# Down projections of three feed-forward groups as seven half-size products in place of eight, on one Trainium2 core

## What is computed

```python
h = rms_norm(x, g_mlp[layer])
x = x + jnp.square(jax.nn.relu(h @ w_up[layer])) @ w_down[layer]
```

## Time and profile before

| | |
|---|---|
| median of 3 runs (lowest to highest) | 1565.25 us (1564.1 to 1566.73) |
| the profiled execution's own time | 1565.43 us |
| its span, first to last instruction | 1563.8 us |
| mean granted TensorE clock | 0.992 of full speed |
| PE, PEld, DVE, ACT, POOL busy | 1515.2, 1422.2, 726.7, 492.3, 117.9 us |
| feed-forward part, in the order of MLP_ORDER | 382 to 789 us (layer 0), 1138 to 1549 us (layer 1) |

### The profile page before, as it was taken

How to read it: one execution, slowest core, us unless ns; L and a number is a source line. 1 busy time by engine, 2 the same in 40 slices (tenths; PEclk the granted TensorE clock), 3 DMA queues, 4 the chain that set the end, 5 groups by cost and what they waited for, 6 DMA issues and landing times.

```text
span 1563.8 us, 33452 instructions
## 1 busy us (share of the span) xinstructions
PE 1515.2 (97%) x13119; PEld 1422.2 (91%) x13119; DVE 726.7 (46%) x1273; ACT 492.3 (31%) x787; POOL 117.9 (8%) x238
## 2 busy tenths in 40 slices
PE   6999999989999999999999999998999999999996
PEld 5999866779999999999999997667999999999996
DVE  4355475635444343343543476774544434334333
ACT  5111154423432132231321115552333313213133
POOL 5310112210000000000010000222000000000000
PEclk9999999999999999999999999999999999999998
DMA  4323477833222223222242227775222222322222
GB/s 132 99 77 83 132 255 246 262 105 90 82 80 86 76 84 91 80 81 83 78 146 84 81 73 248 241 264 156 81 81 82 81 84 77 94 79 83 81 81 75
DMA packets 230949, 178.84 MB, mean 114 GB/s; under 512 B 9320, under 2 KB 202924, under 8 KB 230850
## 3 DMA queue, kind: packets, MB, share of 16 engines
q1 hardware_dynamic: 217154, 137.50, 30.0%
q0 software_dynamic: 13696, 40.00, 8.0%
HBM read 170.20 MB, written 7.26 MB: 113 GB/s over the span
## 4 chain that ended last, share of the span: by engine, by line
PE 90%; DVE 3%; ACT 2%; SPq 2%; issue 2%; DMA 1%; POOLq 0%; POOL 0%; ACTq 0%; DVEq 0%
PE B L1316 71%; PE B L1533 3%; PE B L1342 2%; PE B L1545 2%; PE B L1333 1%; PE B L1627 1%; PE B L1565 1%; PE B L1589 1%; PE B L1576 1%; SPq L382 1%; DMA WR<-in_w_in_even_dram 1%; PE B L1543 1%; PE B L1415 1%; PE B L1486 1%; DVE KP L1162 1%
## 5 line engine op out<-in xcount | busy, mean ns | idle before, releaser
L554 ACT ACTIVATE WH<-WR 128x1024 fp32r<-128x1024 f32 x175 | 184.5, 1054 | 436.6 <-PE B L1316 423.9
L822 DVE TENSOR_TENSOR WL<-WR,WH 128x1024 fp32r<-128x1024 f32 x188 | 230.2, 1224 | 57.6 <-ACT WH L544 28.9
L1316 PE MATMUL B<-ffH,WH 128*128 128x288 f32 x1024 | 218.9, 294 | 0.0
L1316 PE MATMUL B<-ffL,WH 128*128 128x288 f32 x1024 | 218.6, 294 | 0.0
L1316 PE MATMUL B<-ffH,WL 128*128 128x288 f32 x1024 | 217.7, 294 | 0.0
L1316 PE MATMUL B<-H2L,WH 128*128 128x288 f32 x960 | 205.0, 294 | 0.0
L1316 PE MATMUL B<-H2H,WH 128*128 128x288 f32 x960 | 204.7, 294 | 0.0
L1316 PE MATMUL B<-H2H,WL 128*128 128x288 f32 x960 | 204.1, 294 | 0.0
L1316 PE MATMUL B<-HH,WH 128*128 128x288 f32 x832 | 179.9, 298 | 4.2 <-DVE WL L822 2.6
L856 DVE TENSOR_TENSOR X<-B,X 128x288 f32 (+1 forms) x160 | 66.0, 453 | 242.4 <-PE B L1316 242.0
L1316 PE MATMUL B<-HL,WH 128*128 128x288 f32 x832 | 178.6, 296 | 0.0
(11 more groups left out here) (299 smaller groups left out, 1689.3 us busy)
## 6 DMA issues: line engine op xcount, KB each, us to landing
WR<-in_w_up_dram SPq DMA_DIRECT2D x64, 512.0 KB, 4.1
WR<-in_w_down_dram SPq DMA_DIRECT2D x64, 512.0 KB, 3.8
KRX<-in_cache_fox_k_dram SPq DMA_DIRECT2D x48, 256.0 KB, 4.2
WR<-in_w_in_odd_dram SPq DMA_DIRECT2D x24, 512.0 KB, 3.7
KRX<-in_cache_sb_k_dram SPq DMA_DIRECT2D x48, 256.0 KB, 3.8
VR<-in_cache_fox_v_dram POOLq DMA_DIRECT2D x44, 256.0 KB, 4.1
VR<-in_cache_sb_v_dram POOLq DMA_DIRECT2D x44, 256.0 KB, 4.7
WR<-in_w_in_even_dram SPq DMA_DIRECT2D x20, 512.0 KB, 3.9
```

Source lines behind the costliest of these rows:

```text
L554: A(WH[1 - u][:], WR[1 - u][:], ACT.Copy).then_inc(S["w_high"], 1)
L822: V.tensor_tensor(WL[u][:], WR[u][:], WH[u][:].bitcast(F32), ALU.subtract).then_inc(S["w_low"], 1)
L1316: last = M(B[2 * u + h][:, 0:TH], w[u][:, k, :], x[:, k, h * TH:(h + 1) * TH], start=(k == 0 and n == 0), stop=(k == KT - 1 and n == 2))
```

## The change

MLP_ORDER becomes up 0, seven 0, up 1, seven 1, up 2, seven 2, up 3, down 3. A "seven" is a down group done as 2 x 2 block products: two output blocks (m) against the even and odd blocks of the contraction (e) against the two row halves. The eight block products are replaced by seven of sums of blocks (Winograd's form of Strassen's scheme). A seven has NQ = 4 pairs q, each with its own 1 MB of weights; every product is 4 blocks k x 3 partial products = 12 matmuls 128x128 on 128x288 into one bank. Group 3 stays as it was, directly behind its up group.

- Weights of a pair: SP loads them (`load_pair`) into ZR or, for odd q, into both WR buffers (WRP has their address). GpSimd makes four sums of 128x512 per pair (S1 to S4). ScalarE makes the high part (`block_high`, 128x512, seven per pair) and VectorE the low part (`block_low`). The first pair's sums wait until unit 4 of the up group is done.
- Operands: after an up unit VectorE and ScalarE make the blocks and their sums T1 to T4 (`evac_ops`). Even units (u = 0) have T1 to make, odd ones T2, T3 and T4. Both unit-weight cuts of a turn of the loop are in the odd unit's body.
- Results: VectorE adds each product to 1 to 4 blocks of X (`add_product`: 1152, 576, 288, 864, 288, 576 and 288 elements).
- Buffers OPH, OPL and FR lie where ffH and ffL were, ZH, ZL and ZR where HH and HL were. Some semaphores are merged; G_MLP counts (FG + 1) * KT units per layer in place of 2 * FG * KT.

```diff
+        PRODUCTS = [("11", OP_11), ("S1", OP_T1), ("12", OP_21), ("S2", OP_T2), ("S4", OP_22), ("S3", OP_T3), ("22", OP_T4)]
+        def product_bank(q, i):
+            return B[(4 + 7 * q + i) % 8]
...
+                def load_pair(L, grp, q):
+                    Q = pair_no(L, grp, q)
+                    if Q >= 2:
+                        sp.wait_ge(S["block_low"], 7 * (Q - 1))
+                    sp.dma_start((ZR if q % 2 == 0 else WRP)[:, :, :], dn_v[L][grp][:, :, 2 * P * q:2 * P * (q + 1)]
+                                 ).then_inc(S[f"pair_in{q % 2}"], 16)
...
+                    if kind == "seven":
+                        for q in range(1, NQ):
+                            if q == 1:
+                                sp.wait_ge(S["w_low"], g + 2)
+                            load_pair(L, grp, q)
+                        sp.wait_ge(S["block_low"], 7 * (pair_no(L, grp, NQ - 1) + 1))
+                        continue
...
+                        unit_loop(sp, load, g, 4)
...
+                        load_pair(L, grp, 0)
+                        unit_loop(sp, load, g + 4, KT - 4, i0=4)
...
+                        pool.wait_ge(S[f"pair_in{q % 2}"], 16 * (Q // 2 + 1))
+                        if q == 0:
+                            pool.wait_ge(S["unit_done"], G_MLP[L] + grp * KT + 6)
+                        if Q >= 1:
+                            pool.wait_ge(S["block_low"], 7 * (Q - 1) + 2)
+                        g.tensor_tensor(s1, a21, a22, ALU.add).then_inc(S["w_sum"], 1)
+                        if Q >= 1:
+                            pool.wait_ge(S["block_low"], 7 * (Q - 1) + 4)
+                        pool.wait_ge(S["w_sum"], 4 * Q + 1)
+                        g.tensor_tensor(s2, s1, a11, ALU.subtract).then_inc(S["w_sum"], 1)
+                        if Q >= 1:
+                            pool.wait_ge(S["product"], 7 * (Q - 1) + 5)
+                        pool.wait_ge(S["w_sum"], 4 * Q + 2)
+                        g.tensor_tensor(s4, a12, s2, ALU.subtract).then_inc(S["w_sum"], 1)
+                        if Q >= 1:
+                            pool.wait_ge(S["product"], 7 * (Q - 1) + 6)
+                        g.tensor_tensor(s3, a11, a21, ALU.subtract).then_inc(S["w_sum"], 1)
...
+            def block_high(Q, i):
...
+                if Q >= 1:
+                    act.wait_ge(S["product"], 7 * (Q - 1) + i + 1)
+                A(ZH[:, i], block_src(Q, i), ACT.Copy).then_inc(S["block_high"], 1)
...
+                        up_loop(act, body, g + first, first, (KT - 2 - first) // 2)
+                        body(g + KT - 2, KT - 2, NQ - 1, 0, None)
+                        for i in range(5):
+                            block_high(Q, i)
+                        body(g + KT - 1, KT - 1, NQ - 1, 1, None)
+                        block_high(Q, 5)
+                        block_high(Q, 6)
...
+            def evac_ops(L, grp, b0=0, z=None):
...
+                    dve.wait_ge(S["unit_done"], g + 2)
+                    f0 = FR_11 if u == 0 else FR_21
+                    for h in range(2):
+                        done = V.scalar_tensor_tensor(FR[:, f0 + h], B[b0 + 2 * u + h][:, 0:TH], 0.0, R[:, h * TH:(h + 1) * TH], ALU.max, ALU.mult)
+                    done.then_inc(S["relu_scaled"], 1)
+                    dve.wait_ge(S["relu_squared"], i + (m0 + 1))
+                    if u == 0:
+                        V.tensor_tensor(FR[:, FR_T1], FR[:, FR_12], FR[:, FR_11], ALU.subtract).then_inc(S["op_sums"], 1)
+                    else:
+                        V.tensor_tensor(FR[:, FR_T2], FR[:, FR_22], FR[:, FR_T1], ALU.subtract).then_inc(S["op_sums"], 1)
+                        V.tensor_tensor(FR[:, FR_T3], FR[:, FR_22], FR[:, FR_12], ALU.subtract)
+                        dve.wait_ge(S["op_sums"], j * 3 + (3 * j0 + 2))
+                        V.tensor_tensor(FR[:, FR_T4], FR[:, FR_21], FR[:, FR_T2], ALU.subtract).then_inc(S["op_sums"], 1)
+                        low_ops(OP_21, OP_22, FR_21, j, j * 3 + (3 * j0 + 2)).then_inc(S["op_half"], 1)
+                        if more in ("behind", "both"):
+                            cut_low(g + 2, 1)
+                    lo, hi, f = (OP_T1, OP_11, FR_T1) if u == 0 else (OP_T2, OP_T4, FR_T2)
+                    low_ops(lo, hi, f, j, j * 3 + (3 * j0 + (1 if u == 0 else 3))).then_inc(S["evac_dve"], 1)
...
+                        for q in range(NQ):
+                            Q = pair_no(L, grp, q)
+                            for i in range(7):
+                                add_product(Q, q, i)
+                                if q < NQ - 1:
+                                    block_low(Q + 1, i)
+                                elif i == 5:
+                                    cut_low(g, 0)
+                                elif i == 6 and grp + 1 < FG - 1:
+                                    cut_low(g + 1, 1)
...
+                        body(g + KT - 2, KT - 2, NQ - 1, 0, None)
+                        for i in range(5):
+                            block_low(Q, i)
+                        body(g + KT - 1, KT - 1, NQ - 1, 1, None)
+                        block_low(Q, 5)
+                        block_low(Q, 6)
...
+            def seven(L, grp, q, g):
+
+                Q = pair_no(L, grp, q)
+                J = pair_no(L, grp, NQ)
+                for i, (name, op) in enumerate(PRODUCTS):
+                    pe.wait_ge(S["block_low"], 7 * Q + i + 1)
+                    if i == 0 and q == 0:
+                        pe.wait_ge(S["evac_dve"], g + 1)
+                        if Q > 0:
+                            pe.wait_ge(S["product_read"], 7 * Q)
+                    if 7 * q + i >= 8:
+                        pe.wait_ge(S["product_read"], 7 * Q + i - 7)
+                    if q == 0 and name == "12":
+                        pe.wait_ge(S["op_half"], J)
+                    if q == 0 and name == "S2":
+                        pe.wait_ge(S["evac_dve"], g + 2)
+                    for k in range(NQ):
+                        for n, (w, x) in enumerate(((ZH, OPH), (ZH, OPL), (ZL, OPH))):
+                            done = M(product_bank(q, i)[:, 0:TH], w[:, i, k, :], x[:, op, k, :], start=(k == 0 and n == 0), stop=(k == NQ - 1 and n == 2))
+                    done.then_inc(S["product"], 1)
```

More of the change, by code:

```diff
@@ L785, in _ @@
                     last = L == 1 and n == len(MLP_ORDER) - 1
-                    if kind == "down" and grp == FG - 1:
+                    if kind == "seven":
+                        for q in range(1, NQ):
+                            for i in range(7):
+                                block_high(pair_no(L, grp, q), i)
+                        cut_high(g)
+                        if grp + 1 < FG - 1:
+                            cut_high(g + 1)
+                        continue
+                    if kind == "down":
                         for i in range(KT):
                             evac_sq(2 + 2 * L)(g + i, i, i % 2, None if last and i == KT - 1 else "next")
+                    elif grp == FG - 1:
+                        unit_loop(act, evac_up(L, grp), g, KT)
                     else:
-                        body = evac_up(L, grp) if kind == "up" else evac_none
+                        body, Q = evac_ops(L, grp), pair_no(L, grp, 0)
                         if n == 0:
@@ L1319, in unit, with late_chunk_unit @@
                 return body
+            def seven(L, grp, q, g):
+                Q = pair_no(L, grp, q)
+                J = pair_no(L, grp, NQ)
[15 more added lines that the diff above has]
+                    done.then_inc(S["product"], 1)
+            def late_chunk_unit(hi, lo, g):
+                pe.wait_ge(S["w_low"], g + 3)
+                pe.wait_ge(S["evac_dve"], g + 1)
+                for k in range(KT):
+                    if k == KT - 1:
+                        pe.wait_ge(S["evac_dve"], g + 2)
+                    for n, (w, x) in enumerate(((WH, hi), (WH, lo), (WL, hi))):
+                        for h in range(2):
+                            last = M(B[h][:, 0:TH], w[0][:, k, :], x[:, k, h * TH:(h + 1) * TH],
+                                     start=(k == 0 and n == 0), stop=(k == KT - 1 and n == 2))
+                last.then_inc(S["unit_done"], 1)
             def turn_y(k):
@@ L1699, in _ @@
                 g = G_MLP[L]
-                up_end = {}
                 for n, (kind, grp) in enumerate(MLP_ORDER):
+                    if kind == "seven":
+                        for q in range(NQ):
+                            seven(L, grp, q, g)
+                        pe.wait_ge(S["product_read"], 7 * pair_no(L, grp, NQ - 1) + 3)
+                        continue
                     if kind == "up":
```

185 lines of the change are left out of this document (147 added, 38 removed).

## The result

The changed kernel takes 1550.72 us (median of 5 runs, 1548.81 to 1552.88) beside 1565.56 us of the kernel before (5 runs, 1564.1 to 1566.73): a ratio of 0.9903, 95% interval 0.9893 to 0.9914. Forecast were 1545 us and a range of 1532 to 1561. The profiled execution took 1550.72 us, its span is 1549.1 us.

What follows compares the result with a forecast made beforehand. TensorE was taken to set the time. Of 38.1 us saved by fewer matmuls, waits of 0.6, 1.9 and 0.5 us in six groups give back 18, a gain of 20.1: 1545 us, range 1532 to 1561.

Steps and rivals of the forecast that it cites:

- The saving: Six sevens issue 288 fewer matmuls at an unchanged 132.2 ns each: 38.1 us less.
- (b): Start of the seven: TensorE waits 1.3 us for operands plus 0.6 for pair 1's sums colliding with VectorE, 1.9 us per group.
- (a): Unit 6 of the up group: GpSimd's first-pair sums collide with VectorE; wait between 0 and 1.2 us, 0.6 taken.
- (c): End of the seven: the next up unit's weight cut stands behind the sixth product's add; TensorE waits 0.5 us per group.
- Inside a seven: no gap: Per pair of 11.1 us, VectorE needs 9.0 us, ScalarE 4.4 and GpSimd 5.1, so TensorE never waits mid-seven.
- slack of "about 5 us": Inside a seven, VectorE may lag about 5 us, from when low parts are due and banks are reused.
- The path behind it: Seven's end: next up group's loads wait until pair 3 is cut, about 11 us before the end, and need 4.1 us.
- Nothing holds VectorE: Rival: sums never delay VectorE, unit 6 waits 0 and the seven's start 1.3 us; 1538 us, chance 0.27.
- Held whole at the ends: Rival: each sum holds VectorE whole; waits 1.2 at unit 6, 3.7 and 0.5 at seven's ends; 1559.5 us, chance 0.17.
- the 1.3 given as a sign of being right: Sign for the forecast: GpSimd's 96 sums would take near 1.3 us each.
- the 1.8 given as a sign of being wrong: Sign against the forecast: GpSimd sums above 1.8 us.
- the 1.84 at which the gain would have been used up: Slow-sums rival, chance 0.12: from 1.84 us per GpSimd sum the kernel gains nothing; at 2.2 us, 1578 us.

Runs made afterwards that it cites:

- run 1: Changed kernel with GpSimd's four sums left out, their blocks cut from raw block 11 by ScalarE and VectorE instead: 1537.59 us.
- Run 6: Changed kernel with VectorE cutting the next up group's first weights after the fifth add of the last pair, not the sixth: 1547.66 us.
- run 5: Changed kernel with pair 1's sums held until VectorE ends the up group's evacuation, and four weight blocks instead of five before unit 7's evacuation: 1557.78 us.
- run 7: Changed kernel with the edits of run 4, run 5 and Run 6 together: 1554.39 us.
- run 2: Changed kernel with GpSimd's sums replaced by fills of a spare buffer, 1.06 us each, which write and read nothing: 1536.94 us.
- run 4: Changed kernel with the first pair's sums split over two gates, two behind unit 2 and two behind unit 4: 1545.15 us.
- run 9: Changed kernel with the edits of run 4 and Run 6 together, pair 1's sums and blocks unchanged: 1542.38 us.
- run 10: Kernel of run 7 with the last pair's weight blocks made ahead of the later adds in each seven's third pair: 1552.3 us.
- run 11: Kernel of run 9 with four blocks between units 6 and 7 and the last pair's blocks ahead of the adds: 1550.48 us.
- run 3: Changed kernel with every GpSimd sum done twice, one after the other: 1624.27 us.

## Why the prediction was right, point by point

**The saving** of 288 matmuls at 132.2 ns, 38.1 us, stands: neither the waits before each product nor twelve matmuls in one bank slowed them. **(b), the third product**, was put at 1.9 us and is 1.83, but that is luck: its two parts are mis-sized against each other. Without the sums it is 0.73 (run 1), not 1.3; there VectorE ends the evacuation of unit 6 at 432.52, 3.5 us after that unit and not 4.0, and is hardly late to unit 7. And the one block of the five that a sum holds (1.79 us, 0.69 free) adds 1.10, not 0.6.

**(a), unit 6**, was mis-sized: 0.6 taken, the middle of 0 to 1.2; measured 1.13 at five groups. Step by step the working holds: VectorE is held for 1.55 - 0.46 and 2.21 - 1.23, together 2.07 us, and had 0.95 us to spare, which leaves 1.12. What failed is the choice of the middle: at five groups T1 and the cut both came behind a sum that had begun, by 0.05 us in T1's case; at the sixth T1 came first, and the wait is nothing. Each tie goes one way or the other, and no place shows the middle.

**(c), behind the seven**, was 0.5 and is 0.64 to 0.79; it is the same without sums, so it is the add and the cut in line, as put, with a handover more. Run 6 removes it at five of six places.

With the measured waits the sum gives 1565.4 - 38.1 + 20.6 = 1547.9 us; 1.85 of what is left came ahead of the feed-forward part, and the last 1 us is about what steps a little longer than the pace add up to (3.0 us in the feed-forward parts, 1.3 before).

**Inside a seven: no gap** is right in its outcome and wrong in its reason. The 9.0 us of VectorE's work are right (9.15 without sums), but the holds fill the pair to 11.10 of 11.10. The slack of "about 5 us" is thus no reserve: it can be spent once, and runs 5 and 7 spent it. The path behind it was too short as well: pair 3 was to be cut 11 us before the seven ends, and in the trace its last block ends at 475.77, some 7 us before.

**The rivals.** "Nothing holds VectorE" gave 1538, and runs 1 and 2, where nothing does, measured 1537.6 and 1536.9; the changed kernel is not it. "Held whole at the ends" has the right mechanism and the right price at (a), but only one block of (b) is held, not two sums' worth: 1559.5 was too much. The sums took 1.56 us on average, not the 1.3 given as a sign of being right, and the fourth sum of each first pair 1.80 to 2.27, above the 1.8 given as a sign of being wrong. On average they stayed below the 1.84 at which the gain would have been used up; that threshold was drawn for sums slow by themselves, and here VectorE stretches them.

## What to carry to other kernels

Work given to GpSimd was not free of VectorE where both read SBUF, VectorE with both its inputs: look for instructions that are longer than their shape, not for idle time, and price the pair by both timelines. Before removing a wait at the front of a stage, look whether the engine that caused it has room until the stage ends; if it is full, the wait only moves behind the stage, and a longer wait there can cost the clock as well. What paid here were the waits whose removal asks nothing more of the full engine (runs 4 and 6, together run 9).

## What the runs showed of the hardware

A GpSimd sum and a VectorE instruction with two inputs from SBUF hold each other up, in both directions, and the later one does nearly all of its own length only after the one that began first has ended: T1 0.46 to 1.55 us, a weight cut 1.23 to 2.21, a sum 1.29 to 1.80. VectorE's adds from PSUM beside a sum (1.04 to 1.05 us for 864 elements) and anything beside fills by GpSimd of 1.06 us (run 2) kept their lengths.

TensorE standing for 2.58 us was followed by 3 us and more at a granted clock of 0.50. Behind the seven that happened at two of six places in run 7 (waits of 2.4 to 3.1 us), three of six in run 5 (2.4 to 2.8), three of six in run 10 (2.44), one of six in run 11 (the longest, 2.09) and all six in run 3 (4.6 to 5.1). The changed kernel's waits of up to 1.8 us left its feed-forward windows at 1.00. In run 10 the six waits are equal to 0.02 us, so the length of the wait alone does not decide; what does stays open.
